# Two-layer attention plus state-space block: the reciprocal square roots by Sqrt and a reciprocal instead of Ln and Exp, a part of one refinement on GpSimd

## The reference

```
def rms_norm(x, g):                 # EPS = 1e-6; 5 such norms are touched
    y = xf * lax.rsqrt(jnp.mean(xf * xf, axis=-1, keepdims=True) + EPS)
    return (y * g).astype(x.dtype)

def diff_attention(q, k, v, ...):   # second block, 8 heads, two halves of 64 each
    q = rms_norm_2(q.reshape(bsz, L, N_HEADS, 2, HEAD_DIM_2), q_norm_w, RMS_EPS) * (HEAD_DIM_2 ** -0.5)
    k = rms_norm_2(k.reshape(bsz, L, N_HEADS, 2, HEAD_DIM_2), k_norm_w, RMS_EPS)
    ...
    s = jnp.einsum('bqhmd,bkhmd->bhmqk', q_i, k)       # + bias, mask
    p = jax.nn.softmax(s, axis=-1)
    p = p[:, :, 0] - lam * p[:, :, 1]
    return jnp.einsum('bhqk,bkhe->bqhe', p, v)          # then rms_norm_2(o, subln_w)
```

## Time and profile before

| | before |
|---|---|
| time, median of 3 runs | 2631.0 us (2627.27 to 2638.69) |
| profiled execution, its time | 2631.0 us |
| its span, first to last instruction | 2629.0 us |
| PE busy | 2489.3 us (95%) |
| DVE busy | 1799.9 us (68%) |
| ACT busy | 1181.9 us (45%) |
| POOL busy | 406.2 us (15%) |
| mean granted TensorE clock | 0.977 |
| the eight heads of the second block | from 1116.8 us, head i=8 from 1328.1 us |

### The profile page before, as it was taken

One profiled execution on the slowest core, in us unless ns is written; L12 is line 12 of the kernel. 1 busy time (PEld: TensorE's weight loads), 2 busy tenths in 40 slices (PEclk: granted clock), 3 DMA queues, 4 the chain that ended last, 5 costly groups with the idle time before them and its releaser, 6 DMA issues.

```text
span 2629.0 us, 49300 instructions
## 1 busy us (share of the span) xinstructions
PE 2489.3 (95%) x17752; PEld 2324.4 (88%) x17752; DVE 1799.9 (68%) x2565; ACT 1181.9 (45%) x1661; POOL 406.2 (15%) x447
## 2 busy tenths in 40 slices
PE   7999999989999998799988888799999999999999
PEld 7999999889999998788876777699988888888888
DVE  7876766877756668777789999565555555555555
ACT  5354544654444446566642222334444444444443
POOL 3300100122000002100137776110000000000000
PEclk9999999999999999899989999799999999999999
DMA  6655554767555545454534554475677777777774
GB/s 234 212 182 188 183 176 151 224 217 222 176 175 176 175 149 188 160 184 149 178 127 157 157 156 152 147 229 173 191 192 190 185 186 188 185 186 187 184 185 160
DMA packets 212114, 474.03 MB, mean 180 GB/s; under 512 B 20265, under 2 KB 117205, under 8 KB 211777
## 3 DMA queue, kind: packets, MB, share of 16 engines
q1 hardware_dynamic: 182912, 415.29, 52.7%
q0 software_dynamic: 10016, 28.49, 3.7%
q10 hardware_dynamic: 19104, 29.15, 3.4%
HBM read 449.74 MB, written 25.84 MB: 181 GB/s over the span
## 4 chain that ended last, share of the span: by engine, by line
PE 66%; DVE 19%; issue 6%; ACT 4%; DMA 3%; ACTq 0%; DVEq 0%; POOL 0%; POOLq 0%
PE z_ps L1840 12%; PE z_ps L1841 11%; PE z_ps L1842 11%; DVE w_lo L1171 6%; PE z_ps L2123 6%; PE z_ps L2124 6%; PE z_ps L2129 6%; DMA tab_d<-arena 3%; ACT w_hi L650 1%; PE o_ps L1879 1%; PE s_ps L1861 1%; PE o_ps L2158 1%; PE p_ps L2157 1%; PE o_ps L2157 1%; PE o_ps L2156 1%
## 5 line engine op out<-in xcount | busy, mean ns | idle before, releaser
L1171 DVE TENSOR_TENSOR w_lo<-w_raw,w_hi 128x1024 fp32r<-128x1024 f32 x520 | 663.7, 1303 | 299.7 <-ACT w_hi L650 287.5
L1840 PE MATMUL z_ps<-x_hi,w_hi 128*128 128x256 f32 x2816 | 825.8, 293 | 32.6 <-DVE w_lo L1164 14.7
L1841 PE MATMUL z_ps<-x_lo,w_hi 128*128 128x256 f32 x2816 | 806.7, 286 | 0.0
L1842 PE MATMUL z_ps<-x_hi,w_lo 128*128 128x256 f32 x2816 | 806.0, 286 | 0.0
L650 ACT ACTIVATE w_hi<-w_raw 128x1024 fp32r<-128x1024 f32 x520 | 534.4, 1051 | 319.8 <-PE z_ps L1842 311.1
L1840 PEld LDWEIGHTS z_ps<-x_hi,w_hi 128*128 128x128 f32 x2816 | 550.6, 196 | 57.3 <-issue 46.8
L1841 PEld LDWEIGHTS z_ps<-x_lo,w_hi 128*128 128x128 f32 x2816 | 551.2, 196 | 1.3
L1842 PEld LDWEIGHTS z_ps<-x_hi,w_lo 128*128 128x128 f32 x2816 | 550.2, 195 | 0.0
L1730 DVE TENSOR_TENSOR w_lo<-w_raw,w_hi 128x1024 fp32r<-128x1024 f32 x262 | 320.7, 1225 | 315.0 <-ACT w_hi L1019 314.8
L1019 ACT ACTIVATE w_hi<-w_raw 128x1024 fp32r<-128x1024 f32 x262 | 277.7, 1060 | 427.9 <-PE z_ps L2129 270.9
L2123 PE MATMUL z_ps<-w_hi,x_hi 128*128 128x512 f32 x704 | 275.1, 391 | 0.6 <-DVE res L1706 0.6
(11 more groups left out here) (346 smaller groups left out, 3905.6 us busy)
## 6 DMA issues: line engine op xcount, KB each, us to landing
w_raw<-in_w SPq DMA_DIRECT2D x704, 512.0 KB, 4.2
w_raw<-in_w SPq DMA_DIRECT2D x80, 384.0 KB, 4.9
w_raw<-in_w SPq DMA_DIRECT2D x80, 128.0 KB, 2.9
tab_d<-arena ACTq DMA_DIRECT2D x32, 256.0 KB, 4.6
res<-tab_d POOLq DMA_DIRECT2D x32, 256.0 KB, 2.9
sg_d<-arena ACTq DMA_DIRECT2D x32, 128.0 KB, 3.2
arena<-sg_d POOLq DMA_DIRECT2D x16, 256.0 KB, 3.8
arena<-in_dil_bias ACTq DMA_DIRECT2D x12, 256.0 KB, 2.8
```

Source lines behind the costliest of these rows:

```text
L1171: dve.tensor_tensor(w_lo[:, n % RING, :], w_raw[:, n % RING, :], w_hi[:, n % RING, :].bitcast(F32), ALU.subtract).then_inc(w_lo_ready, 1)
L1840: pe.matmul(z, wh, hi[:, kt, :], start=(first and i == 0), stop=False)
L1841: pe.matmul(z, wh, lo[:, kt, :], start=False, stop=False)
L1842: m = pe.matmul(z, wl, hi[:, kt, :], start=False, stop=(last and i == len(kts) - 1))
```

## The change

It does four things. (1) `norm_root` on ACT becomes one Sqrt in place of Ln and Exp, and DVE takes a reciprocal of it (`norm_tail`), for the five 128 x 256 norms. (2) In the second block's attention DVE takes a reciprocal of `nv2` (128 x 512) first, and ACT one Sqrt of it. (3) Of the Newton step there, three products go to POOL (two before and one behind a DVE operation), and DVE keeps one operation. (4) DVE makes `qk_n` at the head of `attn_1`, so behind `split_lo` of job 2 and not ahead of it. The semaphore `norm2_step` counts six steps per head where it counted five.

```diff
@@ POOL, attention(i)
                 load_bias2(h)
+                pool.wait_ge(qk_root, h + 1)
+                pool.tensor_tensor(nt2, ns2, ns2, ALU.mult).then_inc(norm2_step, 1)
+                pool.wait_ge(norm2_step, 6 * h + 3)
+                pool.tensor_tensor(nt2, nt2, nv2, ALU.mult).then_inc(norm2_step, 1)
+                pool.wait_ge(norm2_step, 6 * h + 5)
+                pool.tensor_tensor(nr2, ns2, nt2, ALU.mult).then_inc(norm2_step, 1)
@@ ACT
-            def norm_root(step, root):
+            def norm_root(step):
                 act.wait_ge(norm_step, step)
-                act.activation(ns[:], nv[:], ACT.Ln).then_inc(norm_log, 1)
-                act.wait_ge(norm_log, root)
-                act.activation(nr[:], ns[:], ACT.Exp, scale=-0.5).then_inc(norm_step, 1)
+                act.activation(ns[:], nv[:], ACT.Sqrt).then_inc(norm_sqrt, 1)
             def attn_1(i, prev, prev2, prev3):
                 if prev:
-                    act.wait_ge(norm2_step, 5 * (i - 1) + 1)
-                    act.activation(ns2, nv2, ACT.Ln).then_inc(qk_log, 1)
-                    act.wait_ge(qk_log, i)
-                    act.activation(ns2, ns2, ACT.Exp, scale=-0.5).then_inc(norm2_step, 1)
+                    act.wait_ge(norm2_step, 6 * (i - 1) + 2)
+                    act.activation(ns2, nr2, ACT.Sqrt).then_inc(qk_root, 1)
@@ DVE
-            def norm_tail(dst, step):
+            def norm_tail(dst, step, root):
+                dve.wait_ge(norm_sqrt, root)
+                dve.reciprocal(nr[:], ns[:]).then_inc(norm_step, 1)
                 dve.wait_ge(norm_step, step + 2)
@@ DVE, attn_0 and attn_1
                     dve.tensor_scalar(nv2, s_ps[:], 1.0 / 64, EPS, ALU.mult, ALU.add).then_inc(norm2_step, 1)
+                    dve.wait_ge(norm2_step, 6 * h + 1)
+                    dve.reciprocal(nr2, nv2).then_inc(norm2_step, 1)
                 if prev3:
                     dve.wait_ge(yo_hi, i - 2)
                     dve.tensor_tensor(y_lo[:, i - 3, :], ov, y_hi[:, i - 3, :].bitcast(F32), ALU.subtract).then_inc(yo_lo, 1)
                 if prev:
-                    dve.wait_ge(norm2_step, 5 * h + 2)
-                    dve.scalar_tensor_tensor(out=nt2, in0=nv2, scalar=-0.5, in1=ns2, op0=ALU.mult,
-                                             op1=ALU.mult).then_inc(norm2_step, 1)
-                    dve.wait_ge(norm2_step, 5 * h + 3)
-                    dve.tensor_tensor(nt2, nt2, ns2, ALU.mult).then_inc(norm2_step, 1)
-                    dve.wait_ge(norm2_step, 5 * h + 4)
-                    dve.scalar_tensor_tensor(out=nr2, in0=nt2, scalar=1.5, in1=ns2, op0=ALU.add,
-                                             op1=ALU.mult).then_inc(norm2_step, 1)
-                    dve.wait_ge(norm2_step, 5 * h + 5)
+                    dve.wait_ge(norm2_step, 6 * h + 4)
+                    dve.tensor_scalar(nt2, nt2, -0.5, 1.5, ALU.mult, ALU.add).then_inc(norm2_step, 1)
+
+            def attn_1(i, prev, prev2):
+                if prev:
+                    dve.wait_ge(norm2_step, 6 * (i - 1) + 6)
                     for m in range(2):
                         e = dve.scalar_tensor_tensor(out=qk_n[:, m, :], in0=qk[:, m, :], scalar=vecs[:, m:m + 1],
                                                      in1=nr2[:, m, :], op0=ALU.mult, op1=ALU.mult)
                     e.then_inc(qk_n_ready, 1)
                     dve.wait_ge(qk_n_ready, i)
-
-            def attn_1(i, prev, prev2):
                 if prev2:
```

More of the change, by code:

```diff
@@ L245, in build @@
         norm_step = sem("norm_step")
-        norm_log = sem("norm_log")
+        norm_sqrt = sem("norm_sqrt")
         xsq_step = sem("xsq_step")
@@ L299, in build @@
         norm2_step = sem("norm2_step")
-        qk_log = sem("qk_log")
+        qk_root = sem("qk_root")
         qk_n_ready = sem("qk_n_ready")
@@ L741, in head_period @@
                 if norm:
-                    norm_root(NORM_AT[l] + 1, ROOT_AT[l] + 1)
+                    norm_root(NORM_AT[l] + 1)
                 if prev:
@@ L789, in _ @@
                 if l == 0:
-                    norm_root(NORM_AT[0] + 7, 2)
+                    norm_root(NORM_AT[0] + 7)
                 with act.Fori(m0, HEADS) as h:
@@ L903, in _ @@
             split_hi(P_QKV, 2)
-            norm_root(N0 + 1, ROOT_AT[DEPTH] + 1)
-            norm_root(N0 + 9, ROOT_AT[DEPTH] + 2)
+            norm_root(N0 + 1)
+            norm_root(N0 + 9)
             split_hi(P_QKV, 3)
@@ L1186, in norm_tail, with rstd_of @@
                 dve.tensor_tensor(dst, nr[:], nt[:], ALU.mult).then_inc(norm_step, 1)
-            def rstd_of(sums, dst, step):
+            def rstd_of(sums, dst, step, root):
                 dve.tensor_scalar(nv[:], sums, 1.0 / D, EPS, ALU.mult, ALU.add).then_inc(norm_step, 1)
-                norm_tail(dst, step)
+                norm_tail(dst, step, root)
             def evac(dst, p, c, scale):
@@ L1292, in head_period @@
                     dve.wait_ge(sums_ready, l + 1)
-                    rstd_of(p_ps[:, 0, :], rstd[:], NORM_AT[l])
+                    rstd_of(p_ps[:, 0, :], rstd[:], NORM_AT[l], ROOT_AT[l] + 1)
                     dve.wait_ge(norm_step, NORM_AT[l] + 6)
@@ L1350, in _ @@
                     dve.wait_ge(msums_ready, 1)
-                    rstd_of(v_ps[:, 1, :], rstd_m[:], NORM_AT[0] + 6)
+                    rstd_of(v_ps[:, 1, :], rstd_m[:], NORM_AT[0] + 6, 2)
                 with dve.Fori(m0, HEADS) as h:
@@ L1512, in _ @@
             dve.wait_ge(sums_ready, DEPTH + 1)
-            rstd_of(p_ps[:, 0, :], rstd1, N0)
+            rstd_of(p_ps[:, 0, :], rstd1, N0, ROOT_AT[DEPTH] + 1)
             dve.wait_ge(norm_step, N0 + 6)
@@ L1519, in _ @@
             dve.tensor_scalar(nv[:], nt[:], 1.0 / D, EPS, ALU.mult, ALU.add).then_inc(norm_step, 1)
-            norm_tail(rstd[:], N0 + 8)
+            norm_tail(rstd[:], N0 + 8, ROOT_AT[DEPTH] + 2)
             dve.wait_ge(norm_step, N0 + 14)
```

## The result

| | before | after |
|---|---|---|
| time, median | 2631.4 us (2627.27 to 2638.69, 4 runs) | 2666.6 us (2659.87 to 2669.77, 4 runs) |
| ratio after / before, 95% interval | | 1.0128 [1.0098, 1.0157] |
| profiled execution, its time | 2631.0 us | 2666.6 us |
| mean granted TensorE clock | 0.977 | 0.966 |

The account below looks back on a forecast made before the run. The prediction took a ring of waits through DVE, ACT and PE to bound the second block's heads: 28.7 us for eight heads, 0 for norms, 2.4 for PE's clock, 31 us on 2631.0, so 2662 us, range 2648 to 2680.

Parts of the forecast that it names:

- ring: Second block's heads: mean square, root, Newton, `qk_n`, splits, `osq`, output sums, softmax, PE's turn, next mean square; period 30.40 us.
- the piece: In each head, mean square's start to the evacuation behind `osq`: 9.46 us before, 13.05 predicted, +3.6 per head.
- Reciprocal: DVE's 128 x 512 reciprocal in each head, extrapolated from sizes 256 and 4 to 3.37 us.
- Products: Two 128 x 512 products on POOL while DVE stands still, 1.28 us each, 2.64 with handoff.
- rival of a slow POOL: POOL's head products run at 2.33 us though DVE rests, or POOL answers late: 2672 to 2680 us; chance 12%.
- Scalar operation: The one Newton operation left on DVE in each head: about 0.56 us, 0.60 with handoff.
- Clash: POOL's third product beside DVE's two weight splits in each head: the pair takes 3.46 us, 2.36 without it.
- I take 0.3 per head: Loss in the heads from PE's lower clock after longer waits: 0.3 us per head, 2.4 us in all.
- PE's clock becomes the bound: Rival: PE is slow beyond its spare 1.7 us in every head, another 1.7 per head, 2675 us; chance 12%.
- Norms and table loads: Five other norms priced at 0; new memory-head loads hidden; in heads only the load between Ln and Exp counts.
- The rival that ACT sets the pace: In the heads, 13 table loads and 8 Exps come off, 21.7 us, giving 2609 us; chance 4%.
- Hidden anyway: Rival: DVE's 4.7 us of waits before splits in the heads absorb the 3.6, giving 2631 us; chance 8%.

Follow-up runs that it names:

- e3: The changed kernel with the three Newton operations back on DVE and POOL's products taken out; 2650.7 us, ratio 1.0062 to the kernel before.
- e4: The changed kernel with `qk_n` ahead of the weight splits of job 2 again, so DVE waits for POOL's third product; 2669.8 us, ratio 1.0127 to the kernel before.
- e5: The changed kernel with 26 useless matmuls on PE ahead of the output sums in heads 1 to 7; 2658.1 us, ratio 1.0083 to the kernel before.
- e1: The kernel before with only the five 128 x 256 norms changed to Sqrt and reciprocal, heads as before; 2639.9 us, ratio 1.0002 to the kernel before.
- e6: The changed kernel with the job 2 weight splits moved into DVE's wait for POOL, ACT's `w_hi` ahead of Sqrt; 2660.9 us, ratio 1.0086 to the kernel before.

## Why the prediction held, point by point

The forecast was 2662 us with the mechanism of a ring on which DVE, ACT and POOL answer one another; 2666.6 was measured, inside the range. The profiled execution is 35.6 us above that of before, 31 were expected. Of the prediction's own sums one is off: the steps that it adds up put DVE at the splits at 1244.7 us and not 1244.8, which changes nothing.

The steps of the piece, from start to start in the timelines above:

| step | predicted | measured |
|---|---|---|
| mean square | 0.73 | 0.72 |
| reciprocal 128 x 512, with handoff | 3.37 | 3.39 |
| Sqrt, with handoff | 0.66 | 0.72 |
| two products on POOL | 2.64 | 2.44 |
| scalar operation | 0.60 | 0.34 |
| the two splits beside the third product | 3.46 | 3.36 |
| `qk_n` and `osq` | 1.59 | 1.57 |
| sum | 13.05 | 12.54 |

- *Reciprocal.* The line through two sizes held (3353 ns), and the price of the first half of the change rests on it: 3.39 + 0.72 in place of 0.03 + 2.58 for handoff, Ln, load and Exp, 1.50 more. e3 measures the balance, with `qk_n` moved, as 1.36.
- *Products.* Both were taken at 1.28. The second was (1.29). The first squares one tile, and took 1.04 in every head. None was slow while DVE rested, so the rival of a slow POOL falls.
- *Scalar operation.* Mis-sized most, 0.60 for 0.34: it took 0.43 and not 0.56, and the split behind it started before the end that the profile gives it.
- *Clash.* Sized well (3.43 and 3.46 for 3.46), and shown by e4, where the third product ran apart and the pair took 2.36, and by the single splits (1.22 and 2.30). The Trainium skill, "SBUF — State Buffer", section "SBUF: two separate sides", has one of the two engines hold a shared port pair for the whole instruction; e4 and the changed kernel (1.28 + 2.36 = 3.64 apart, 3.43 together) agree with that up to 0.2 us.
- *Clock.* The step "I take 0.3 per head" is the one that was too small. In a full period it is 0.66, in the first 2.1. e5 shows it, by taking it away. The rows from head i=2, on which the 0.3 rested, had 3.4 us at 0.50; with the longer wait it is 6.8 us, of which 5.6 lie in work, and 6.6 in the first period. The rival "PE's clock becomes the bound" was thus right on what happens (PE is late before its turn in all seven periods) and wrong on its size, 1.7 per head.
- *Two errors that offset.* The pieces grew by 25.0 us in the eight heads, where 28.7 were priced: 3.7 too dear. The rest of the seven periods grew by 5.9 us, where 2.4 were priced for the clock: 3.5 too cheap. 25.0 + 5.9 = 30.9 us, as in the table above. That the heads meet the 31 so closely is luck.
- *Head i=8.* Predicted to lose the same as the others: 3.2 us.
- *Norms and table loads.* Priced at 0, measured 1.0002 in e1. Of the table loads in the heads only the one between Ln and Exp was on the path, as priced; after the change ACT waits 7.82 us before 871, where it was 3.43. The rival that ACT sets the pace falls.
- *Hidden anyway.* DVE's waits before later splits did not take the loss in. They grew, from 1.95 us to 2.59 before the splits of job 1.
- *What stays open.* 5.0 us of the 35.9 of the span are outside the heads. 2.1 of them are at the start and within the scatter there. The other 2.9 fall mostly into the state-space stage behind the heads (333.6 us, was 331.0). The mean granted clock was 0.88 there, and 0.90 before; but e1, with the heads of before, also had 0.88, and 332.6. The four profiles without products on POOL in the heads have 331.0 to 332.6, the six with them 332.8 to 334.0. Each is one execution, and whether a part of this belongs to the change was not tried.

## What to carry to other kernels

Price an edit on the ring of waits that it stands in, from the start of one instruction to the start of the next over every engine it visits; busy time and table loads saved on an engine that waits are worth nothing. Here ACT's work fell by 23 us and the kernel became 35 us longer, because what replaced it stood on the ring. Do not count on a GpSimd product and a VectorE operation with two inputs overlapping until a row of the trace shows it. Before a product goes to GpSimd while another engine waits for it, price it at its full length there: 1.04 to 1.29 us here, for 0.69 on VectorE. When a wait of TensorE grows, look at the granted clock behind it: the loss is paid where the engine had only a little time to spare. And a gap in a queue is free only if what fills it does not depend on a later release, and if no table load hides in the wait ahead of it.

## What the runs showed of the hardware

- Useless matmuls in place of a wait of TensorE took 5.6 us off the seven periods (e5): the granted clock was 1.00 in a period in which it was 0.90 without them.
- A GpSimd product of 128 x 512 with the same tile as both inputs took 1.04 us, with two different tiles 1.29. Beside two weight splits of VectorE they took turns (e6): the first product kept its time (1.07) and the split beside it took 2.06 for 1.22, then the second product took 2.15.
- GpSimd started its third product 0.54 us after the end of the product before it, for a DVE operation of 0.43 in between: the way from GpSimd to DVE and back cost 0.1 us more than the operation itself.
- Where Ln and Exp followed each other in the kernel before, a table load of 1.28 us stood between them in each head.
